# Two block-diagonal products on TensorE, rewritten from full-width accumulations to column tiles of 32 output rows

## The reference, cut to what matters

```python
# indexer scores of a sample: every cached position l gets a score from 8 heads
dots = jnp.einsum('bqhd,bld->bqhl', qi, ki) * (IDX_DIM ** -0.5)
s = jnp.einsum('bqhl,bqh->bql', jax.nn.relu(dots), wi).astype(jnp.float32) * (N_IDX_HEADS ** -0.5)
...
_, sel = lax.top_k(sc, topk)          # sample: 256 of 2049 positions
...
# attention scores of a sample over its 256 chosen keys
s = jnp.einsum('bqngd,bqknd->bqngk', qg, k_sel).astype(jnp.float32) * (HEAD_DIM ** -0.5)
```

## Time and profile before

| | |
|---|---|
| median of 3 runs | 1488.75 us (1480.33 to 1491.7) |
| the profiled execution, its own time | 1478.28 us |
| its span, first to last instruction | 1476.5 us |
| TensorE busy | 1372.5 us, 93% of the span |
| VectorE busy | 815.3 us, 55% |
| ScalarE busy | 488.9 us, 33% |
| mean granted TensorE clock | 0.971 of full speed |

### The profile page before, as it was taken

One profiled execution on the slowest core, in us unless ns is written; L12 is line 12 of the kernel. 1 busy time (PEld: TensorE's weight loads), 2 busy tenths in 40 slices (PEclk: granted clock), 3 DMA queues, 4 the chain that ended last, 5 costly groups with the idle time before them and its releaser, 6 DMA issues.

```text
span 1476.5 us, 26124 instructions
## 1 busy us (share of the span) xinstructions
PE 1372.5 (93%) x9828; PEld 1215.8 (82%) x9828; DVE 815.3 (55%) x1836; ACT 488.9 (33%) x971; POOL 190.6 (13%) x238
## 2 busy tenths in 40 slices
PE   6989978997999999999996989689989999999997
PEld 4855744697999999999976547458989999999997
DVE  2448787437655665822353587764467555566223
ACT  5212136545322222422351121564442222225221
POOL 1000454005000000000020005620140000000001
PEclk9999978999999999999998999799989999999999
DMA  9970112021222222222269401020212222222231
GB/s 316 234 123 0 36 40 86 1 86 44 101 86 99 85 91 94 88 109 79 81 252 159 91 3 70 23 68 8 99 53 100 86 92 93 85 93 97 87 113 59
DMA packets 51940, 133.28 MB, mean 90 GB/s; under 512 B 6559, under 2 KB 29951, under 8 KB 44783
## 3 DMA queue, kind: packets, MB, share of 16 engines
q1 hardware_dynamic: 49039, 119.52, 27.2%
q0 software_dynamic: 2816, 12.62, 2.5%
HBM read 119.94 MB, written 12.82 MB: 90 GB/s over the span
## 4 chain that ended last, share of the span: by engine, by line
PE 72%; DVE 12%; DMA 6%; issue 4%; SPq 2%; ACT 2%; POOL 1%; DVEq 0%; POOLq 0%; ACTq 0%
PE ps L883 56%; DMA W<-in_w_pairs 3%; PE ps L870 2%; DMA moR<-in_idx_pages,part_of 2%; PE ps L987 2%; PE ps L1049 2%; PE ps L1168 2%; SPq L594 2%; PE ps L1147 1%; DVE moR L1783 1%; DVE SEL L1888 1%; DVE yR L1957 1%; PE ps L1040 1%; DVE SEL L1919 1%; DVE W_r L2151 1%
## 5 line engine op out<-in xcount | busy, mean ns | idle before, releaser
L883 PE MATMUL ps<-moR_r,W_r 128*128 128x260 f32 x1376 | 285.1, 283 | 0.0
L883 PEld LDWEIGHTS ps<-moR_r,W_r 128*128 128x128 f32 x1376 | 215.1, 188 | 0.0
L883 PE MATMUL ps<-hT_r,QZC_r 128*128 128x260 f32 x864 | 178.1, 283 | 0.0
L883 PE MATMUL ps<-moR_r,SQ_r 128*128 128x260 f32 x704 | 147.4, 284 | 1.8 <-DVE W_r L2151 1.8
L883 PE MATMUL ps<-hT_r,SQ_r 128*128 128x260 f32 x704 | 145.8, 281 | 0.0
L883 PE MATMUL ps<-moR_r,QZC_r 128*128 128x260 f32 x672 | 139.3, 284 | 1.1 <-DVE hT_r L2173 0.8
L883 PEld LDWEIGHTS ps<-hT_r,QZC_r 128*128 128x128 f32 x864 | 135.0, 188 | 0.0
L883 PEld LDWEIGHTS ps<-moR_r,SQ_r 128*128 128x128 f32 x704 | 110.8, 189 | 2.2 <-DVE W_r L2151 2.2
L883 PEld LDWEIGHTS ps<-hT_r,SQ_r 128*128 128x128 f32 x704 | 110.5, 188 | 0.0
L2245 DVE TENSOR_TENSOR SEL<-ps,rstd 128x520 f32<-128x520 f32 x44 | 30.8, 699 | 141.6 <-PE ps L883 137.6
L883 PEld LDWEIGHTS ps<-moR_r,QZC_r 128*128 128x128 f32 x672 | 105.3, 189 | 2.3 <-DVE hT_r L2173 2.3
(11 more groups left out here) (366 smaller groups left out, 3054.7 us busy)
## 6 DMA issues: line engine op xcount, KB each, us to landing
W<-in_w_gates SPq DMA_DIRECT2D x44, 512.0 KB, 3.2
W<-in_w_vals SPq DMA_DIRECT2D x44, 512.0 KB, 3.2
W<-in_w_downs SPq DMA_DIRECT2D x16, 1024.0 KB, 4.9
W<-in_w_pairs SPq DMA_DIRECT2D x12, 1024.0 KB, 7.8
pages_by_slot<-moR SPq DMA_DIRECT2D x8, 1024.0 KB, 5.9
yR<-pages_by_slot SPq DMA_DIRECT2D x16, 512.0 KB, 18.2
W<-in_w_outs SPq DMA_DIRECT2D x8, 1024.0 KB, 4.9
W<-in_w_downs SPq DMA_DIRECT2D x16, 384.0 KB, 5.6
```

What stands on the lines that cost most here:

```text
L883: last = mm(ps[:, banks[f], 0:HT], w(k), half(x(k), f), start=(k == 0 and n == 0), stop=(k == nk - 1 and n == 2))
```

## The change

In both functions the output rows are cut into tiles of 32, and each tile receives only the samples whose rows lie in it. In `page_products` tile c holds the rows of samples 2c and 2c+1, so that two products instead of eight are accumulated; in `sample_scores` tile c holds samples 4c to 4c+3, four products. The loops are turned so that successive matmuls go to different tiles. The number of matmuls, the moving operands and the columns they stream stay as they were; the stationary operand shrinks from 128 (or 64) to 32 columns.

```diff
                     for a in range(2):
-                        for b in range(NB):
-                            last = mm(ps[:, 6 + a, :], qM[:, P * b:P * b + P],
-                                      IK[:, b, 4 * a:4 * a + 4, :].rearrange("p j r -> p (j r)"),
-                                      start=(b == 0), stop=(b == NB - 1))
+                        for i in range(2):
+                            for c in range(4):
+                                b, r = 2 * c + i, slice(32 * c, 32 * c + 32)
+                                last = mm(ps[r, 6 + a, :], qM[:, P * b + 32 * c:P * b + 32 * c + 32],
+                                          IK[:, b, 4 * a:4 * a + 4, :].rearrange("p j r -> p (j r)"),
+                                          start=(i == 0), stop=(i == 1))
                         last.then_inc(sdot_mm.sem, 1)
...
-                    for b in range(NB):
-                        last = mm(ps[0:64, 3, 0:2 * P], qbz[:, b, :], KTS[:, 2 * b:2 * b + 2, :].rearrange("p t k -> p (t k)"),
-                                  start=(b == 0), stop=(b == NB - 1))
+                    for i in range(NB // 2):
+                        for c in range(2):
+                            b, r = 4 * c + i, slice(32 * c, 32 * c + 32)
+                            last = mm(ps[r, 3, 0:2 * P], qbz[:, b, r], KTS[:, 2 * b:2 * b + 2, :].rearrange("p t k -> p (t k)"),
+                                      start=(i == 0), stop=(i == NB // 2 - 1))
                     last.then_inc(qs_mm.sem, 1)
```

## The result

The changed kernel is slower: 1510.28 us (1509.48 to 1512.62, 4 runs) against 1490.17 us for the kernel before (1480.33 to 1491.7, 4 runs), ratio 1.0166, 95% interval 1.0117 to 1.0215. (The ratio is that of the fast runs of each kernel; the quotient of the two medians is 1.0135.) The time lies above the range I gave (1478 to 1498). The profiled execution took 1510.85 us with a span of 1509.1, against 1478.28 and 1476.5.

What follows compares the result with a forecast made beforehand. VectorE's key search, nearly level with TensorE's path, was taken to bound the first count, and VectorE the search loop. Per layer, 1.8 us lost there cancelled 1.8 gained in the sample scores: 0.0, so the median, 1489 us, range 1478 to 1498.

Steps and rivals of the forecast that it cites:

- The page products' 3.5 us: Page products on TensorE: four tiles work fully beside each other, so 13.73 us per layer become 3.5.
- The rival that nothing overlaps: Matmuls of different column tiles follow each other as before; page products keep 13.7 us, time stays 1489 us; chance 0.18.
- loads stand before their products: Each weight load waits for the product in flight: +3.5 us page products, +1.8 sample scores per layer, 1499 us; chance 0.06.
- The cover: Before the first count, VectorE's 19.5 us key search hides the saving: 0.3 of 10.2 us gained, 9.5 us wait.
- The fall of the clock in the wait: TensorE's wait before the first count, 6 us or more, ends with its granted clock at half.
- The return of the clock: In the threshold search after the first count: clock back 4.3 to 5.5 us after restart, by dot step 13.
- The term of +1.8 us per layer: Search loop after the wait: a short half-clock spell makes the second count's answer 1.8 us late, 0.3 gain included.
- the clock stays down: Half clock lasts in the search loop: about three rounds, 1496 us, chance 0.06; five or more, over 1% slower, 0.04.
- That rival's price: Half clock through all twelve search rounds: 1.9 us each, 22.8 us per layer, +42 us in total, 1531 us.
- The sample scores: Sample scores on TensorE, uncovered: two tiles overlap, 3.60 us become 1.8, gaining 1.8 us per layer in full.
- The base: Starting time the summed terms were added to: 1488.75 us, the median of the kernel before's runs, spread 1480.33 to 1491.7.

Runs made afterwards that it cites:

- the padded kernels: Dot products over 128 rows using zero-filled key copies: changed kernel 1474.27 us, kernel before 1472.54 us, changed kernel plus ten unused products 1470.57 us.
- the last experiment: Kernel before, unchanged, profiled again at 1495.06 us; of 26 runs beside it, 18 took 1474.75 to 1480.65 us, 8 took 1488.76 to 1493.26.
- the second profile: Another profile of the unchanged kernel before: 1495.06 us, layer 0's loop at full clock, layer 1's at half from 867.2 us.
- the burst: Changed kernel plus five unused full-width products behind the first count in each layer: 1491.81 us, ratio 1.0037.
- full-width quarter: Kernel before, no column tiles, page products of only two of the eight samples, at full width: 1518.37 us, ratio 1.0243.
- dots over two heads: Changed kernel with dot products from step 11 on over all 128 rows, adding two heads' dots (another result): 1477.82 us, ratio 0.9945.

## Why the prediction was wrong

**The page products' 3.5 us: right.** The tiles overlap fully, 3.57 us against 13.8. The rival that nothing overlaps, or that loads stand before their products, is out. The rule of the Trainium skill (TensorE: Matmul & The Clock Gate, Part 3, "What overlaps and what doesn't") that a load goes beside products in flight only where the row group differs is not borne out here: all four tiles use all rows, and 32 products of 592 ns each pass in 3.57 us.

**The cover: right.** The wait came out at 9.37 us against 9.5, for the line named. From the first page product to the first count the layer gained 0.7 us (23.48 before, 22.76 after), where 0.3 had been put; the prediction's own times, a count at 124.5 instead of 125.03, make it 0.5.

**The fall of the clock in the wait: right**, at 115.2, 2.2 us into it (3.3 to 3.8 in the rows of before).

**The return of the clock: this step failed.** "Dot step 13 finds the clock back up" was carried over from the rows where it came back 4.3 and 5.5 us after a restart. Those restarts were line 883, dense products of 128 rows. In the loop here each step has a dot product of 64 rows and a count, and the clock didn't return for its whole length. The term of +1.8 us per layer was +15.0. What came is the rival "the clock stays down", which I gave 0.04 for five rounds or more with the reason that the dot steps follow each other without a break. They did so, and it was not enough. I had the row that spoke for it: after 201.40 the clock took 11.9 us, with TensorE listed as busy in about 9 of them. Where the dot products have 128 rows the term comes out: 1.7 and 2.1 us in the two layers of the padded kernels.

**That rival's price** was too high for its own case, 22.8 us per layer. The 12 rounds took 49.74 us (122.42 to 172.16) where 34.02 went before (125.03 to 159.05), so 15.7 more, 1.3 per round instead of 1.9: a round at half clock is 3.82, not 4.4, because no part of it doubles: the four pooling products take 1.89 us for 1.07, the dot product 1.58 for 0.84, the count 0.35 for 0.28; and the rounds of 512 columns already took 3.0 at full clock, which I had put at 2.50 throughout.

**The sample scores: right**, 1.75 against 1.8; VectorE's wait went from 4.69 to 3.09, forecast 2.9.

**The base.** I added the sum to the median. The runs before are a mixture: by the two groups of the last experiment most executions keep the clock in both loops, and some lose one, at some 13 us (9.8 of them between the first page product and the first query product in the second profile). The forecast's span of runs was, by this, the same mechanism at work in the kernel before, and I took it for scatter. The high base made the miss look smaller: the result lies 21 us above the forecast, while between the two profiled executions, the one before with both loops at full clock, there are 32.6 us.

Shown: the loss is the granted clock in the loop (the burst restores the old rounds), it comes from the short page products and not from the tiles (full-width quarter), and with 128 rows in the dot products the clock comes back. Not settled: what decides, in a given execution at full clock, whether the 64-row loop loses it; and whether the rows count as such, or through the shorter steps they bring (at full clock 1.3 us instead of 1.7 for a step of 256 columns). Padding together with only the sample scores in tiles was not run; the parts make it the next thing to try.

## What to carry to other kernels

A piece of TensorE work that the chain names may be standing in front of another engine's path of equal length; shorten it and you buy a wait, and what matters then is at what clock the following stretch runs. When you estimate how fast the clock returns, take it from a restart with the same kind of products: half-height products in a loop paced by another engine may keep the half clock to the end of the loop. Filling the unused rows with zeros took three more ScalarE instructions per layer here and brought the kernel before to a ratio of 0.9926 (0.9895 to 0.9956), all its runs between 1469.4 and 1475.7 us. Of the 7.0 us between the medians 5.9 are shorter dot steps at full clock; that none of its runs shows a lost loop (0.967 to 0.972) comes on top.

## What the runs showed of the hardware

- Four column tiles of 32, all on the same rows, ran fully beside each other: 32 records in 3.57 us, 112 ns each, close to the 110 ns of their loads; two tiles 3.60 to 1.85.
- A gap of 2.34 to 2.50 us ahead of the 64-row loop cost the clock in both layers of two profiles: 0.8 and 1.1 us after work had restarted in layer 0, up to 0.1 us before it in layer 1. After 2.13 and 2.14 us ahead of the 128-row loop it fell in one layer and not in the other. One of 0.77 or 0.78 us was not followed by a fall at the restart, in either layer of the one profile that has it.
- The 64-row loop stayed at half clock for 50 us while listed as busy throughout; with 128 rows the clock was back 4.1 and 6.5 us (dots over two heads, layers 0 and 1) and 5.8 and 6.6 us (padded) after the restart.
- A dot product of 128 rows is no slower than one of 64: at full clock the next product starts after 0.73 us instead of 0.84 (384 columns), and eight steps of 256 columns without waits take 10.57 us instead of 13.51.
